# Two routers, the blocks beyond the experts' first, and the closing stage of a two-block transformer kernel, rewritten together

## The reference

```python
# first block: each expert takes its 128 best tokens
aff = softmax(u @ w_router)                  # (1024, 16)
gates, idx = top_k(swapaxes(aff), 128)
# second block, hier_moe: best of 4 groups, then the 2 best of its 8 experts
g_w, g_idx = top_k(softmax(h @ w_group + b_group), 1)
e_w, e_idx = top_k(softmax(e_sel), 2)
weights = g_w * e_w / sum(e_w)
# the 2048 assignments are put into blocks of 128 that each belong to one expert
y_buf = each block: (silu(xb @ w_gate[e]) * (xb @ w_up[e])) @ w_down[e]
x = x + g2 * (the two weighted rows of y_buf of each token)
return rms_norm(x, gain)
```

## Time and profile before

| what | value |
|---|---|
| median of 3 runs (lowest, highest) | 4900.81 us (4894.11, 4903.95) |
| profiled execution: its own time, its span | 4908.46 us, 4906.8 us |
| PE busy, DVE busy, ACT busy, POOL busy | 86%, 32%, 16%, 8% of the span |
| first router stage | about 1331 to 1431 us |
| second router stage | about 3797 to 3908 us |
| further blocks | about 4639 to 4823 us |
| last stage | about 4824 us to the end |

### The profile page before, as it was taken

The page is one execution under the profiler, slowest core; times in us unless marked ns, Lnnn a source line. Parts: engine busy times, 40 slices in busy tenths (PEclk is TensorE's granted clock), DMA queues, the critical chain, the costliest instruction groups (busy, mean ns, idle before and its releaser), DMA issues. The chain is left out here.

```text
span 4906.8 us, 43985 instructions
## 1 busy us (share of the span) xinstructions
PE 4213.9 (86%) x15266; PEld 2372.8 (48%) x15266; DVE 1584.1 (32%) x3374; ACT 774.9 (16%) x1759; POOL 407.3 (8%) x386
## 2 busy tenths in 40 slices
PE   5799999987869999999999819987988499999851
PEld 3466666665424444444444314456764444444320
DVE  4577777773350000000000053329433100000004
ACT  2233333331100000000000011111541010010000
POOL 0111111110000000000000000015000100000001
PEclk8899999998869999999999959988899599999875
DMA  6211111102379898888888531100112289999744
GB/s 254 51 36 38 38 38 34 38 22 111 144 280 339 305 312 310 306 309 311 303 308 313 187 141 28 26 5 1 66 57 101 52 320 336 332 335 336 266 156 173
DMA packets 440267, 872.94 MB, mean 178 GB/s; under 512 B 95345, under 2 KB 139201, under 8 KB 433977
## 3 DMA queue, kind: packets, MB, share of 16 engines
q1 hardware_dynamic: 412201, 779.00, 45.5%
q0 software_dynamic: 20800, 73.57, 4.5%
q10 hardware_dynamic: 7120, 18.49, 1.0%
HBM read 798.54 MB, written 72.47 MB: 178 GB/s over the span
## 5 line engine op out<-in xcount | busy, mean ns | idle before, releaser
L1814 PE MATMUL moe_gbank<-moe_ring,moe_xT 128*128 128x512 f32 x1536 | 679.5, 595 | 3.9 <-ACTq L1870 3.9
L1832 PE MATMUL moe_acc<-moe_ring,moe_hidT 128*128 128x512 f32 x1536 | 675.1, 592 | 1.8 <-DVEq L1929 1.1
L1814 PE MATMUL moe_ubank<-moe_ring,moe_xT 128*128 128x512 f32 x1536 | 675.1, 592 | 0.0
L1904 DVE TENSOR_TENSOR moe_hid<-moe_sg,moe_ubank 128x512 f32<-128x512 f32 x96 | 66.0, 688 | 1658.4 <-PE moe_ubank L1814 1658.4
L921 PE MATMUL gdn_pbank<-mix_xT,gdn_w 128*128 128x512 f32 (+1 forms) x1280 | 542.0, 557 | 2.2 <-PEq L815 2.2
L1814 PEld LDWEIGHTS moe_gbank<-moe_ring,moe_xT 128*128 128x128 f32 x1536 | 293.3, 191 | 373.5 <-issue 370.3
L1832 PEld LDWEIGHTS moe_acc<-moe_ring,moe_hidT 128*128 128x128 f32 x1536 | 288.2, 190 | 347.1 <-issue 347.1
L1814 PEld LDWEIGHTS moe_ubank<-moe_ring,moe_xT 128*128 128x128 f32 x1536 | 284.5, 190 | 322.4 <-issue 322.4
L921 PEld LDWEIGHTS gdn_pbank<-mix_xT,gdn_w 128*128 128x128 f32 x1280 | 229.4, 194 | 162.4 <-issue 154.4
L1875 ACT ACTIVATE moe_sg<-moe_gbank 128x512 f32<-128x512 f32 x96 | 57.3, 597 | 1547.2 <-PE moe_gbank L1814 1547.2
L2050 PE MATMUL proj_abank<-mix_yT,proj_wq 128*128 128x512 f32 x416 | 180.8, 592 | 0.6 <-PE proj_abank L2050 0.6
(11 more groups left out here) (510 smaller groups left out, 5057.5 us busy)
## 6 DMA issues: line engine op xcount, KB each, us to landing
moe_ring<-in_moe_w_gate SPq DMA_DIRECT2D x64, 2048.0 KB, 7.8
moe_ring<-in_moe_w_up SPq DMA_DIRECT2D x64, 2048.0 KB, 8.6
moe_ring<-in_moe_w_down SPq DMA_DIRECT2D x64, 2048.0 KB, 7.7
moe_ring<-in_w_gate SPq DMA_DIRECT2D x32, 2048.0 KB, 9.2
moe_ring<-in_w_up SPq DMA_DIRECT2D x32, 2048.0 KB, 9.8
moe_ring<-in_w_down SPq DMA_DIRECT2D x32, 2048.0 KB, 10.6
front_wt<-in_w_mod SPq DMA_DIRECT2D x24, 1024.0 KB, 13.7
route_wt<-in_w_ada SPq DMA_DIRECT2D x24, 1024.0 KB, 14.7
```

Of the source, the lines that this page charges most:

```text
L1814: last = nc.tensor.matmul(bank[:], xT[:, k, :], w[:, k * 512:(k + 1) * 512], start=(k == 0), stop=(k == KD - 1))
L1832: last = nc.tensor.matmul(acc[j][:], hidT[:, k, :], w[:, k * D + j * 512:k * D + (j + 1) * 512], start=(f == 0 and k == 0), stop=(f == NF ...
L1904: nc.vector.tensor_tensor(hid[:], sg[:], ubank[:], ALU.mult).then_inc(u_free, 1)
```

## The change

In the first router the operands change places: the router's 16 columns are stationary and 512 tokens move, 16 products in all; ACT copies the two 16x512 results to SBUF (into `work[1]`, not yet in use), and PE turns them into `lg` with 8 transposes.

```diff
+                for j in range(2):
+                    for k in range(KD):
+                        last = nc.tensor.matmul(aT[j][:], wr[:, k, :], uT[:, k, j * 512:(j + 1) * 512], start=(k == 0), stop=(k == KD - 1))
+                    last.then_inc(lT_full, 1)
                 for t in range(NT):
-                    for k in range(KD):
-                        last = nc.tensor.matmul(lg[:, t * E1:(t + 1) * E1], uT[:, k, t * P:(t + 1) * P], wr[:, k, :], start=(k == 0), stop=(k == KD - 1))
+                    if t % 4 == 0:
+                        pe.wait_ge(lT_out, t // 4 + 1)
+                    last = nc.tensor.transpose(lg[:, t * E1:(t + 1) * E1], work[1][:, t * P:(t + 1) * P], ident[0:E1, 0:E1])
                 last.then_inc(lg_ready, 1)
...
+                for j in range(2):
+                    act.wait_ge(lT_full, j + 1)
+                    nc.scalar.activation(work[1][:, j * 512:(j + 1) * 512], aT[j][:], ACT.Copy).then_inc(lT_out, 1)
```

```diff
+                for j in range(2):
+                    for k in range(KD):
+                        last = nc.tensor.matmul(lT[j][:], wr[:, k, :], hT[:, k, j * 512:(j + 1) * 512], start=(k == 0), stop=(k == KD - 1))
+                    last.then_inc(lT_full, 1)
                 for t in range(NT):
-                    for k in range(KD):
-                        last = nc.tensor.matmul(lps[:, t, :], hT[:, k, t * P:(t + 1) * P], wr[:, k, :], start=(k == 0), stop=(k == KD - 1))
+                    if t % 4 == 0:
+                        pe.wait_ge(lT_out, t // 4 + 1)
+                    last = nc.tensor.transpose(lps[:, t, :], ls[:, t * P:(t + 1) * P], ident[0:NE, 0:NE])
...
+                nc.tensor.matmul(rps[:], strict[:], O[:], start=True, stop=False)
                 for b in range(NT):
-                    last = nc.tensor.matmul(cps[:], ones, O[:, b, :], start=(b == 0), stop=(b == NT - 1))
+                    last = nc.tensor.matmul(rps[:, b + 1:NT + 1, :], ones, O[:, b:b + 1, :].broadcast_to([P, NT - b, E2]), start=False, stop=(b == NT - 1))
                 last.then_inc(r_full, 1)
+                for n in range(KT):
+                    pe.wait_ge(pos_hot, n + 1)
+                    pe.wait_ge(blk_hot, n + 1)
+                    last = nc.tensor.matmul(ips[:], at_pos[:, n, :], at_blk[:, n, :], start=(n == 0), stop=(n == KT - 1))
+                last.then_inc(i_full, 1)
...
-                for k in range(2):
-                    for t in range(NT):
-                        nc.gpsimd.indirect_dma_start(out=tok_d, out_offset=bass.IndirectOffsetOnAxis(ap=dest[:, k, t:t + 1], axis=0), in_=tok[:, t:t + 1], in_offset=None).then_inc(scattered, 16)
-                        n += 1
-                pool.wait_ge(scattered, 16 * n)
-                with nc.allow_non_contiguous_dma("one word for each slot"):
-                    pool.dma_start(idxT, tok_v).then_inc(taken, 16)
-                pool.wait_ge(taken, 16)
+                pool.wait_ge(blk_ready, 1)
+                for n in range(KT):
+                    nc.gpsimd.tensor_scalar(at_blk[:, n, :], iota[:, 0:NBLK], blk[:, n:n + 1], tokf[:, n % NT:n % NT + 1], ALU.is_equal, ALU.mult).then_inc(blk_hot, 1)
...
+                gkb = gk[:].unsqueeze(3).broadcast_to([P, NT, NG, EPG])
+                do(V.tensor_tensor(big[:], ev, gkb, ALU.mult))
...
+                for k, e in enumerate((e1, e2)):
+                    do(V.tensor_tensor(O12[:, k].rearrange("p t (g e) -> p t g e", g=NG), e[:].unsqueeze(2).broadcast_to([P, NT, NG, EPG]), gkb, ALU.mult))
+                do(V.tensor_tensor(O[:, 0:NT, :], O12[:, 0], O12[:, 1], ALU.add)).then_inc(o_ready, 1)
+
+                O16 = O12[:].rearrange("p k t e -> p (k t) e")
+                sel16 = sel[:].rearrange("p k t e -> p (k t) e")
+                do(V.tensor_tensor(sel16, O16, over(iota[:, 0:E2], E2, KT), ALU.mult))
+                do(V.tensor_reduce(own[:], sel16, AX.X, ALU.add))
...
+                for k in range(2):
+                    V.tensor_tensor(sel[:, k], O12[:, k], rps[:, 0:NT, :], ALU.mult)
+                do(V.tensor_tensor(over_m[:], bc(rps[:, NT, :], NM), over(thr[:], NM, E2), ALU.is_gt))
+                V.tensor_reduce(rank[:], sel16, AX.X, ALU.add)
+                do(V.tensor_reduce(nx[:], over_m[:], AX.X, ALU.add))
                 do(V.tensor_tensor_scan(inc[:], nx[:], zr[:], 0.0, ALU.add, ALU.add))
+                V.tensor_tensor(Jm[:], bc(rank[:], NM), over(thr[:], NM, KT), ALU.is_ge)
                 do(V.tensor_tensor(exc[:], inc[:], nx[:], ALU.subtract))
...
+                V.tensor_reduce(J[:], Jm[:], AX.X, ALU.add)
+                do(V.tensor_tensor(sel16, O16, over(exc[:], E2, KT), ALU.mult))
+                V.scalar_tensor_tensor(out=pos[:], in0=J[:], scalar=-float(P), in1=rank[:], op0=ALU.mult, op1=ALU.add)
+                do(V.tensor_reduce(first[:], sel16, AX.X, ALU.add))
+                do(V.scalar_tensor_tensor(out=first[:], in0=first[:], scalar=float(E2 - 1), in1=J[:], op0=ALU.add, op1=ALU.add))
+                do(V.tensor_tensor(first[:], first[:], own[:], ALU.subtract))
+                do(V.scalar_tensor_tensor(out=first[:], in0=J[:], scalar=0.0, in1=first[:], op0=ALU.is_gt, op1=ALU.mult))
+                do(V.tensor_tensor(blk[:], first[:], own[:], ALU.add)).then_inc(blk_ready, 1)
+                for n in range(KT):
+                    V.tensor_scalar(at_pos[:, n, :], iota[:], pos[:, n:n + 1], None, ALU.is_equal).then_inc(pos_hot, 1)
+                do(V.scalar_tensor_tensor(out=rank[:], in0=blk[:], scalar=float(P), in1=pos[:], op0=ALU.mult, op1=ALU.add))
+                do(V.tensor_copy(dest.rearrange("p k t -> p (k t)"), rank[:]))
...
+                dve.wait_ge(i_full, 1)
+                do(V.tensor_copy(idxT, ips[:]))
```

```diff
+        def load_gate(sp, b):
+
+            e = sp.value_load(ebk[0:1, bass.ds(b, 1)], min_val=0, max_val=E2 - 1)
+            sp.dma_start(wg[:].rearrange("p (k n) -> p k n", k=KD), w_gate[bass.ds(e, 1), :, :].rearrange("a (k p) n -> p (a k) n", p=P)).then_inc(w0, 16)
+
+        def gather(pool, b, count):
+
+            nc.gpsimd.tensor_copy(gidx[:], idxT[:, bass.ds(b + E2, 1)]).then_inc(idx_ready, 1)
+            pool.wait_ge(idx_ready, count)
+            nc.gpsimd.indirect_dma_start(out=xg[:], out_offset=None, in_=rows, in_offset=bass.IndirectOffsetOnAxis(ap=gidx[:], axis=0)).then_inc(gathered, 16)
+
+        with nc.Block() as block:
+            @block.sync
+            def _(sp):
+                load_gate(sp, 0)
+
+            @block.gpsimd
+            def _(pool):
+                nc.gpsimd.memset(idxT[:, E2 + EXTRA:E2 + EXTRA + 1], 0)
+                gather(pool, 0, 1)
+                pool.wait_ge(gathered, 16)
+
+        with nc.Block() as block:
+            @block.sync
+            def _(sp):
+                sp.sem_clear(idx_ready)
...
-                        sp.dma_start(wg[:].rearrange("p (k n) -> p k n", k=KD), w_gate[sel, :, :].rearrange("a (k p) n -> p (a k) n", p=P)).then_inc(w0, 16)
                         sp.dma_start(wu[:].rearrange("p (k n) -> p k n", k=KD), w_up[sel, :, :].rearrange("a (k p) n -> p (a k) n", p=P)).then_inc(w1, 16)
                         sp.dma_start(wd[:].rearrange("p (k n) -> p k n", k=4), w_down[sel, :, :].rearrange("a (k p) n -> p (a k) n", p=P)).then_inc(w2, 16)
+                        sp.wait_ge(g_full, 1)
+                        sp.sem_clear(w0)
+                        load_gate(sp, b + 1)
...
                     @block.gpsimd
                     def _(pool):
-                        nc.gpsimd.tensor_copy(gidx[:], idxT[:, bass.ds(b + E2, 1)]).then_inc(idx_ready, 1)
-                        pool.wait_ge(idx_ready, 1)
-                        nc.gpsimd.indirect_dma_start(out=xg[:], out_offset=None, in_=rows, in_offset=bass.IndirectOffsetOnAxis(ap=gidx[:], axis=0)).then_inc(gathered, 16)
-                        pool.wait_ge(gathered, b * 16 + 16)
+                        pool.wait_ge(x_full, 1)
+                        gather(pool, b + 1, 1)
+                        pool.wait_ge(gathered, b * 16 + 32)
...
                     def _(sp):

                         for n in names:
-                            if n != "gathered":
+                            if n not in ("gathered", "w0"):
                                 sp.sem_clear(sems[n])
...
         with nc.Block() as block:
             @block.sync
             def _(sp):
+                sp.wait_ge(w0, 16)
```

```diff
+                for t in range(NB):
+                    sp.dma_start(x[t][:], res_rows[t]).then_inc(x_loaded[t], 16)
                 sp.dma_start(gb[:], row_view(gate)).then_inc(loaded, 16)
                 sp.dma_start(nb[:], row_view(gain)).then_inc(loaded, 16)
                 for t in range(NT):
-                    if t >= 2:
-                        sp.wait_ge(stored[t % 2], 16 * (t // 2))
-                    sp.dma_start(x[t % 2][:], res_rows[t]).then_inc(x_loaded[t % 2], 16)
+                    sp.wait_ge(o_ready, t + 1)
```

(37 more changed lines are left out.)

153 lines of the change are left out of this document (57 added, 96 removed).

## The result

The changed kernel takes 4791.86 us, the median of 4 runs (4783.71 to 4794.89), where the kernel before took 4897.6 us beside it (4 runs, 4894.11 to 4903.95). The ratio is 0.9776, its 95% interval 0.9764 to 0.9787: faster, by 105.7 us as the medians go. The forecast was 4794 and 106.9. Two later executions, one of the kernel before (14235.35 us, mean clock 0.298) and one of e11 (8945.79 us, 0.489), ran slow throughout and are left out of the medians. The profiled execution took 4788.9 us, with a span of 4786.9 and a mean clock of 0.931.

What follows compares the result with a forecast made beforehand. PE is busy most of the span, so only stretches where it waits or does omittable work give time. Gains 11.0 + 54.6 + 22.4 + 18.9 = 106.9 us give 4801.6, less 7.65 to the median: 4794 us, range 4780 to 4818.

Steps and rivals of the forecast that it cites:

- case A: Whole kernel: the four parts gain as priced, giving 4794 us, own range 4783 to 4806; chance 0.63.
- Router product: Both routers: 32 wide records take 16.3 us, DVE starts 17.9 us after PE instead of 27.5, saving 9.6 us each.
- Rival B: Both routers: clock stays down because only 16 or 36 array columns hold weights, products take 27.5 us; 4818 us, chance 0.10.
- DVE up to the one-hots: Second router: fewer, wider DVE instructions cut this stretch from 11.85 us to 8.4 us.
- The one-hots: Second router: GpSimd 0.28 us each, 4.5 in all, under PE's 6.9; with the copy of `idxT` 8.4 us.
- The rule on shared access: Second router: DVE and GpSimd one-hots shut each other out, 16 pairs take 8.3 us, stage ends about 1.5 us later.
- Further blocks: Further blocks: prefetched rows and gate weights save 8.5 us in three steps, less block changes; 22.4 us, 19 to 25.5.
- Rival D: Further blocks: prefetch buys nothing because steps wait for weights, not rows; +22 us, 4816 us, chance 0.04.
- Last stage: Last stage: shorter DVE work, 44.4 us from 68.3, with a later start, saves 18.9 us, 16 to 25.
- C: Unseen prices at upper ends: GpSimd one-hots at 1.04 us, or the lock, and a late last stage; 4796 to 4808, chance 0.14.
- E: Bounds fall well together: row vectors early, block changes free, clock up early; 4782 us and below, chance 0.06.
- F: Second router: GpSimd's TENSOR_SCALAR with two pointer operands far slower than any row, kernel slower than before; chance 0.03.

Runs made afterwards that it cites:

- e11: Changed kernel with e6's last stage, e9's split, e10's products, and three and two extra products ahead of the routers; 4789.28 us, ratio 0.9769.
- e8: Changed kernel with unread extra products ahead of both router products, four in the first router, eight in the second; one execution, 4798.88 us.
- e7: Changed kernel where DVE waits for all of GpSimd's one-hots before making its own; second-router stage 55.3 us against 49.5.
- e6: Changed kernel, last stage with row vectors ahead of residual loads and SP asking for each residual one tile later; one execution, 4795.28 us.
- e9: Changed kernel with GpSimd making only the even block one-hots and DVE the odd ones; the next stage gains 0.6 us.
- e10: Changed kernel with twelve extra unread products in the state-space stage ahead of attention, where PE waits for DVE; median 4791.83 us.

## Why the prediction was right

The forecast, 4794 with 0.63 on case A, holds by its sum and in the main by its terms. That it came within some 2 us is in part luck: the further blocks brought 3.0 us more than was said and the last stage 1.9 less, and inside the second router 3.0 us lost on the one-hots were nearly made up by three terms that were taken too high. Step by step:

- *Router product*: 16.3 us was said, 16.28 and 15.68 measured; DVE 17.9 behind, measured 17.41 and 16.84. Worth 9.6 in each, measured 10.1 and 10.7. e8 bears out that the part above 14.0 is the clock. Rival B (the clock stays down because only 16 or 36 columns of the array hold weights) is refuted by the same rows: it gave 27.5 us.
- *DVE up to the one-hots*: 8.4 us, measured 8.4 (3799.20 to 3807.60). Counting: 5.7, measured 5.7. Up to `blk`: 6.0, measured 5.6.
- *The one-hots*: the step that failed. It took 0.28 us for GpSimd's instruction of 47 columns, between 0.18 and 1.04, "because 47 columns are near the former". Measured are 0.643 beside DVE and 0.52 alone. The point between the two rows was chosen by the number of columns, and neither row has this form; how much of the 0.52 is fixed and how much goes with the columns was not measured, since it ran at one width only. The sign for it stood in the text ("above 0.43 us each, so that PE waits for them") and came true: the list is ready 11.4 us behind `blk` and not 8.4, 3.0 us lost. The product (1.1), `blk` (0.4) and a shorter change of stages (1.4 us from the copied list to GpSimd's next instruction, where 2.5 was taken) made it up to 0.6 us.
- *The rule on shared access*. The cost of company was put at 1.5 us by an estimate from the Trainium skill, SBUF — State Buffer, "Who interferes with whom", for the one-hots of the two engines shutting each other out; e7 measures 1.9. The size agrees by chance, for of the 1.9 only some 0.8 fall to the six one-hots beside DVE's (3.88 us against 6 x 0.52), the rest to the four beside DVE's two-input passes, which the estimate left out. The same section says that a DVE instruction with two inputs from SBUF contends with a GpSimd instruction that reads SBUF, and this trace agrees: 0.83 us against 0.52. Exclusion for the whole length of DVE's 3.45 us is not what these rows show: GpSimd makes more than five one-hots in that time, and DVE itself lost only 0.22 us in sixteen. Whether DVE's one-hots ran in the two-port mode at all, which is the rule's condition, no run here shows: in e7 one takes 0.28 us (mean 279 ns), near the 0.29 of other forms at 128 columns.
- *Further blocks*: 22.4 said, 25.4 measured, at the upper end of 19 to 25.5. The changes of blocks cost 2.1 us at the start, as said (2.2). The mis-sized term is the clock: "I expect the lower clock still" ahead of each step gave no credit for the shorter idle stretch, but the gate product goes from 9.94, 10.12 and 10.20 us to 9.21, 8.84 and 8.65, 3.6 us over three steps, and the steps come 34.5 to 35.8 us apart, not 35.5 throughout. Rival D (weights hold the step) is refuted: PE's gate product still starts 1.17 us behind its turn and is released by ACT's copies.
- *Last stage*: 18.9 said, 17.0 measured. The late start, +5.3 by loads and gathers in turns, was +5.6 (10.3 to 15.9 us); the sum took 5.0 for it, a slip. From DVE's first pass to its last it is 45.2 us and not 44.4, though a tile without waits takes 5.2 us and not 5.5; and from the last pass to the end it is 0.6 us more than before, which had no term. The step that failed is the loads' half of "Later loads and gathers have four tiles' time and stay hidden": SP's queue holds a wait for a store's landing in front of each load, and that costs DVE 2.9 us. e6 takes most of it back (1.2 left). The half on gathers holds: DVE waits for none between tiles, although the issue of four of them on GpSimd grows from 0.94 to 1.74 to 1.98 us.
- *The time from the profiled execution to the median*. The prediction took the kernel before's profile as 7.65 us above the median and carried that over. No reason stood behind it, and it turned out well: by the two profiles alone the change would look worth 119.6 us. The long attention stage is large enough to make the offset; that it made it was not measured, since the other executions have no trace.

Rivals C, E and F: C's upper end for GpSimd (1.04) was not reached, but half of the distance to it was; E's row vectors came late, not early; F is excluded by the 0.64 us.

## What to carry to other kernels

Price a small GpSimd instruction by a row of its own form; here neither a copy's row nor the number of columns gave its time. Where two engines and PE work through a list, work out what each needs for the whole of it, the work queued behind the list on the same engine too: taking the slowest away moved the wait to the next queue (e9: 3.3 us less on PE, 0.6 at the end). A DMA queue that waits for its own store before it issues the next load makes the load late; ask for it one tile later in the queue. Before two profiles are subtracted, look for a stage that the change does not touch: here one such stage differs by 9 us by itself.

## What the runs showed of the hardware

- The attention stage has two lengths, 199 and 208 us, with the same code: the granted clock is back at its full level about 15 or about 35 us behind the stage's start, with PE busy 84% or more in each window of 10 us, and full clock in PE's preceding wait (e10) changed nothing.
- A GpSimd TENSOR_SCALAR of 128x47 takes 0.52 us alone, 0.65 beside DVE's TENSOR_SCALAR of 128 columns, 0.83 beside DVE's TENSOR_TENSOR of 480 columns.
- An indirect gather's issue on GpSimd takes 0.94 us with DVE idle. In the last stage the four issues that begin while DVE is in a SCALAR_TENSOR_TENSOR of 1024 columns take 1.74 to 1.98 us; the four that begin just ahead of a TENSOR_TENSOR of 1024 columns take 0.93 to 1.00. Whether the form or the order decides was not tried.
- After 6.4 us without work PE's first products lose 1.6 to 2.2 us to the lower clock (8.65 and 9.21 against 7.03 for 16 records), after 14.84 us 2.9.
